# Weighting the experts' rows on their way out and scattering them with adding transfers

## The reference, cut to what matters

```
x   = layernorm(alpha * x + mixer(x))
gp, g  = best of 4 groups (softmax);  e1, e2 = best two of the 4 experts of g, weights ep
combine[token, expert] = gp * ep          # two non-zero entries per token
h   = silu(x @ w_gate[e]) * (x @ w_up[e]) * combine[:, e]
y   = sum over e of h @ w_down[e]
x   = layernorm(alpha * x + y)
```

## Time and profile before

| | |
|---|---|
| median of three executions | 2062.17 us |
| the profiled execution, and its span | 2069.1 us, 2067.4 us |
| PE, VectorE, ACT, POOL busy | 84%, 55%, 43%, 32% |
| read from and written to DRAM | 226.01 MB, 23.23 MB |
| experts, layer 1 and layer 2 | 423.3 to 616.3 us, 1064 to 1258 us |
| second norm, layer 1 and layer 2 | 616.3 to 652 us, 1258.8 to 1296 us |

### The profile page before, as it was taken

The page is one execution under the profiler, slowest core; times in us unless marked ns, Lnnn a source line. Parts: engine busy times, 40 slices in busy tenths (PEclk is TensorE's granted clock), DMA queues, the critical chain, the costliest instruction groups (busy, mean ns, idle before and its releaser), DMA issues. The chain is left out here.

```text
span 2067.4 us, 22445 instructions
## 1 busy us (share of the span) xinstructions
PE 1734.3 (84%) x7990; PEld 1332.7 (64%) x7990; DVE 1138.7 (55%) x1697; ACT 890.2 (43%) x1326; POOL 652.5 (32%) x346
## 2 busy tenths in 40 slices
PE   6999896859971999987859991899697689999997
PEld 4876533748851876732747871788277478888885
DVE  4926565459956745654458985580555424233242
ACT  3246565238853245654327872323635331111111
POOL 2336522112210434632201210343532024444441
PEclk9999997969985999997879996899689899999998
DMA  5201111079944311020147972320000222222211
GB/s 187 74 33 42 42 41 60 15 279 350 372 186 172 108 40 43 1 82 0 62 199 302 376 294 110 144 102 3 20 1 1 82 87 105 94 102 101 93 69 51
DMA packets 40476, 233.84 MB, mean 113 GB/s; under 512 B 9316, under 2 KB 9700, under 8 KB 20660
## 3 DMA queue, kind: packets, MB, share of 16 engines
q1 hardware_dynamic: 31012, 215.44, 27.6%
q0 software_dynamic: 9216, 16.80, 2.2%
q10 hardware_dynamic: 144, 0.26, 0.1%
HBM read 226.01 MB, written 23.23 MB: 121 GB/s over the span
## 5 line engine op out<-in xcount | busy, mean ns | idle before, releaser
L258 PE MATMUL bank<-XS,WS 128*128 128x512 f32 x864 | 200.7, 395 | 11.6 <-DVE WS L383 10.0
L2336 POOL TENSOR_TENSOR WS<-ring,WS 128x2048 fp32r<-128x2048 f32 x31 | 149.6, 4825 | 188.3 <-ACT WS L2324 188.3
L258 PEld LDWEIGHTS bank<-XS,WS 128*128 128x128 f32 x864 | 164.6, 191 | 47.3 <-DVE WS L383 10.5
L1342 PE MATMUL bank<-WS,XS 128*128 128x512 f32 x768 | 188.9, 403 | 1.1 <-DVE XS L1462 1.1
L2357 PE MATMUL bank<-XS,WS 128*128 128x512 f32 x768 | 174.9, 389 | 3.0 <-DVEq L2386 3.0
L2324 ACT CAST WS<-ring 128x2048 fp32r<-128x2048 f32 x31 | 59.3, 1913 | 271.7 <-PE bank L2357 144.0
L2375 PE MATMUL bank<-WS,US 128*128 128x512 f32 x768 | 174.7, 389 | 0.0
L1342 PEld LDWEIGHTS bank<-WS,XS 128*128 128x128 f32 x768 | 146.0, 194 | 32.2 <-DVE XS L1462 1.9
L2357 PEld LDWEIGHTS bank<-XS,WS 128*128 128x128 f32 x768 | 144.1, 188 | 33.1 <-DVEq L2386 3.2
L2375 PEld LDWEIGHTS bank<-WS,US 128*128 128x128 f32 x768 | 144.1, 188 | 29.9
L1687 PE MATMUL bank<-XS,WS 128*128 128x512 f32 (+1 forms) x600 | 139.1, 395 | 3.1 <-POOLq L1738 3.1
(11 more groups left out here) (506 smaller groups left out, 3488.3 us busy)
## 6 DMA issues: line engine op xcount, KB each, us to landing
raw<-in_w_exp SPq DMA_DIRECT2D x16, 2048.0 KB, 13.8
DN<-in_w_exp SPq DMA_DIRECT2D x32, 1024.0 KB
ring<-in_w_ff SPq DMA_DIRECT2D x32, 1024.0 KB, 4.8
raw<-in_w_in SPq DMA_DIRECT2D x20, 1024.0 KB, 4.8
GU<-in_w_exp SPq DMA_DIRECT2D x8, 2048.0 KB, 16.1
XT<-in_w_exp SPq DMA_DIRECT2D x8, 2048.0 KB, 16.4
ring<-in_w_in SPq DMA_DIRECT2D x12, 1024.0 KB, 4.8
raw<-in_w_out SPq DMA_DIRECT2D x8, 1024.0 KB, 5.0
```

What stands on the lines that cost most here:

```text
L258: last = pe.matmul(m.ps[g % 8][:, :], WS[:, i % 2, hw, at:at + P], XS[:, hx, k, :], start=(step == 0), stop=(step == 3 * KD - 1))
L1342: last = pe.matmul(m.ps[2 + e % 2][:, :], r.XS[:, e % 2, hx, 4 * half + k, :], r.WS[:, half, hw, k * S:(k + 1) * S], start=(half == 0 and ...
L2336: pool.tensor_tensor(f.WS[:, q % 2, 1, :], f.ring[:, q % 4, :], f.WS[:, q % 2, 0, :].bitcast(F32), ALU.subtract).then_inc(w_low, 1)
```

## The change

The router computes for each token and expert the weight (0 where the expert is not used) and stores it in VAL as a rounded part and a remainder; VAL grows from two to four numbers, and the target row of the scatter is now the token itself. `index` yields one integer column and, in a second VectorE instruction, the weight WT of each gathered row. ACT brings the down product home multiplied by WT. The scatter adds into `mixed_dram`, which is now 512 rows and starts as a copy of X; since two experts may touch one row, each scatter waits until the one before has landed. The copies of X (`x_rows` as before, and `mixed_dram`) are issued by SP in `norm_stage` as the tiles are finished, all four tiles to `x_rows` first, and POOL waits for all eight before its first gather. The second norm loads 512 KB per tile straight into X and has no additions.

```diff
 norm_stage, SP:
+            for dram in (m.rows_dram, m.mixed_dram):
+                for t in range(NT):
+                    sp.wait_ge(finished, t + 1)
+                    sp.dma_start(dram[t * P:(t + 1) * P, :], m.X[:, t, :]).then_inc(m.rows_out, 16)
 norm_stage, VectorE, finish(t):
-                link(dve.tensor_tensor(m.X[:, t, :], m.X[:, t, :], ln.GB[:, D:2 * D], ALU.add))
+                dve.tensor_tensor(m.X[:, t, :], m.X[:, t, :], ln.GB[:, D:2 * D], ALU.add).then_inc(finished, 1)
 router:
-        @block.sync
-        def _(sp):
-            for t in range(NT):
-                sp.dma_start(m.rows_dram[t * P:(t + 1) * P, :], m.X[:, t, :]).then_inc(copied, 16)
-            sp.wait_ge(copied, 16 * NT)
...
-            link(dve.tensor_tensor(by_group(r.SEC[:, :, :]), every_group(r.h2[:, :, :]), hot_group, ALU.mult))
-            link(dve.tensor_tensor(r.VAL[:, :, :, 1], m.TOK[:, 1, :]..., r.SEC[:, :, :], ALU.add))
...
+            link(dve.tensor_tensor(r.h1[:, :, :], r.h1[:, :, :], wide(r.gm[:, :]), ALU.mult))
+            link(dve.tensor_tensor(r.h2[:, :, :], r.h2[:, :, :], wide(r.m2[:, :]), ALU.mult))
+            link(dve.tensor_tensor(r.h1[:, :, :], r.h1[:, :, :], r.h2[:, :, :], ALU.add))
+            link(dve.tensor_tensor(by_group(r.WV[:, :, :]), every_group(r.h1[:, :, :]), hot_group, ALU.mult))
+            link(dve.tensor_copy(r.VAL[:, :, :, 1], r.WV[:, :, :]))
+            link(dve.tensor_tensor(r.VAL[:, :, :, 2], r.WV[:, :, :], r.VAL[:, :, :, 1].bitcast(F32), ALU.subtract))
+            link(dve.tensor_copy(r.VAL[:, :, :, 3], r.VAL[:, :, :, 0].bitcast(F32)))
 experts, POOL:
             def scatter(e):
                 pool.wait_ge(ye_low, e + 1)
                 pool.wait_ge(ye_up, e + 1)
-                pool.indirect_dma_start(out=m.mixed_dram, out_offset=...(ap=r.TB[:, e, 1:2], axis=0),
-                                        in_=r.YE[:, e % 2, :], in_offset=None, bounds_check=2 * S - 1, oob_is_err=False)...
+                if e:
+                    pool.wait_ge(ye_out[(e - 1) % 2], 16 * ((e - 1) // 2 + 1))
+                pool.indirect_dma_start(out=m.mixed_dram, out_offset=...(ap=r.TB[:, e, 0:1], axis=0),
+                                        in_=r.YE[:, e % 2, :], in_offset=None, bounds_check=S - 1, oob_is_err=False,
+                                        compute_op=ALU.add)...
+            pool.wait_ge(m.rows_out, 16 * 2 * NT)
             gather(0)
 experts, PE:
-                    pe.wait_ge(indexed, e)
+                    pe.wait_ge(weighed, e)
...
-                    last = pe.matmul(m.ps[7][:, 2 * e:2 * e + 2], r.HOT[:, e % 2, t, :], r.VAL[:, t, e, :], ...)
+                    last = pe.matmul(m.ps[7][:, 4 * e:4 * e + 4], r.HOT[:, e % 2, t, :], r.VAL[:, t, e, :], ...)
 experts, ACT:
             def out_home(e):
+                act.wait_ge(weighed, e + 1)
...
-                    act.copy(r.YE[:, e % 2, half * S:(half + 1) * S], m.ps[5 + half][:, :])...
+                    act.mul(r.YE[:, e % 2, half * S:(half + 1) * S], m.ps[5 + half][:, :], r.WT[:, e:e + 1])...
 experts, VectorE:
-                dve.tensor_scalar(r.TB[:, e, :], m.ps[7][:, 2 * e:2 * e + 2], float(NOWHERE), None, ALU.add).then_inc(indexed, 1)
+                dve.tensor_scalar(r.TB[:, e, :], m.ps[7][:, 4 * e:4 * e + 1], float(NOWHERE), None, ALU.add).then_inc(indexed, 1)
+                dve.reduce_sum(r.WT[:, e:e + 1], m.ps[7][:, 4 * e + 1:4 * e + 3], AX.X).then_inc(weighed, 1)
 combine_norm:
-                sp.dma_start(r.MIX[:, t, :], m.mixed_dram.rearrange("(s c) d -> s (c d)", c=2)[t * P:(t + 1) * P, :])...
+                sp.dma_start(m.X[:, t, :], m.mixed_dram[t * P:(t + 1) * P, :])...
...
-                for c, weight in enumerate((r.gm, r.m2)):
-                    link(dve.scalar_tensor_tensor(out=m.X[:, t, :], in0=r.MIX[:, t, c * D:(c + 1) * D], scalar=weight[:, t:t + 1], in1=m.X[:, t, :], ...))
```

More of the change, by code:

```diff
@@ L1151, in router @@
 def router(nc, m, r):
-    names = ("dve_step", "hot_ready", "rank_done", "total_done", "exp_in", "exp_done", "copied")
-    with stage(nc, "router", *names) as (block, (dve_step, hot_ready, rank_done, total_done, exp_in, exp_done, copied)):
-        @block.sync
-        def _(sp):
-            for t in range(NT):
-                sp.dma_start(m.rows_dram[t * P:(t + 1) * P, :], m.X[:, t, :]).then_inc(copied, 16)
-            sp.wait_ge(copied, 16 * NT)
+    names = ("dve_step", "hot_ready", "rank_done", "total_done", "exp_in", "exp_done")
+    with stage(nc, "router", *names) as (block, (dve_step, hot_ready, rank_done, total_done, exp_in, exp_done)):
         @block.gpsimd
@@ L1304, in scatter @@
                 pool.wait_ge(ye_up, e + 1)
-                pool.indirect_dma_start(out=m.mixed_dram, out_offset=bass.IndirectOffsetOnAxis(ap=r.TB[:, e, 1:2], axis=0),
-                                        in_=r.YE[:, e % 2, :], in_offset=None, bounds_check=2 * S - 1, oob_is_err=False).then_inc(ye_out[e % 2], 16)
+                if e:
+                    pool.wait_ge(ye_out[(e - 1) % 2], 16 * ((e - 1) // 2 + 1))
+                pool.indirect_dma_start(out=m.mixed_dram, out_offset=bass.IndirectOffsetOnAxis(ap=r.TB[:, e, 0:1], axis=0),
+                                        in_=r.YE[:, e % 2, :], in_offset=None, bounds_check=S - 1, oob_is_err=False,
+                                        compute_op=ALU.add).then_inc(ye_out[e % 2], 16)
+            pool.wait_ge(m.rows_out, 16 * 2 * NT)
             gather(0)
@@ L1371, in table_of @@
                 if e:
-                    pe.wait_ge(indexed, e)
+                    pe.wait_ge(weighed, e)
                 for t in range(NT):
                     pe.wait_ge(hot_row, e * NT + t + 1)
-                    last = pe.matmul(m.ps[7][:, 2 * e:2 * e + 2], r.HOT[:, e % 2, t, :], r.VAL[:, t, e, :], start=(t == 0), stop=(t == NT - 1))
+                    last = pe.matmul(m.ps[7][:, 4 * e:4 * e + 4], r.HOT[:, e % 2, t, :], r.VAL[:, t, e, :], start=(t == 0), stop=(t == NT - 1))
                 last.then_inc(table_done, 1)
@@ L1416, in out_home @@
                         act.wait_ge(ye_out[e % 2], 16 * (e // 2))
-                    act.copy(r.YE[:, e % 2, half * S:(half + 1) * S], m.ps[5 + half][:, :]).then_inc((ye_low, ye_up)[half], 1)
+                    act.mul(r.YE[:, e % 2, half * S:(half + 1) * S], m.ps[5 + half][:, :], r.WT[:, e:e + 1]).then_inc((ye_low, ye_up)[half], 1)
             def part_high(e):
@@ L1535, in _ @@
             for t in range(NT):
-                sp.dma_start(r.MIX[:, t, :], m.mixed_dram.rearrange("(s c) d -> s (c d)", c=2)[t * P:(t + 1) * P, :]).then_inc(mix_in[t], 16)
+                sp.dma_start(m.X[:, t, :], m.mixed_dram[t * P:(t + 1) * P, :]).then_inc(mix_in[t], 16)
                 if t == 0:
@@ L1555, in _ @@
                 dve.wait_ge(mix_in[t], 16)
-                for c, weight in enumerate((r.gm, r.m2)):
-                    link(dve.scalar_tensor_tensor(out=m.X[:, t, :], in0=r.MIX[:, t, c * D:(c + 1) * D], scalar=weight[:, t:t + 1], in1=m.X[:, t, :], op0=ALU.mult, op1=ALU.add))
                 for half in range(2):
@@ L1573, in square @@
                 act.wait_ge(finished, t + 1)
-                act.activation(r.MIX[:, t, 0:D], m.X[:, t, :], ACT.Square, accum_out=m.SS[:, t:t + 1]).then_inc(squared, 1)
+                act.activation(r.MIX[:, t, :], m.X[:, t, :], ACT.Square, accum_out=m.SS[:, t:t + 1]).then_inc(squared, 1)
             for t in range(NT):
@@ L2583, in build @@
                         r.SEC = sb(nc, c3, "SEC", P, NT, NE)
-                        r.VAL = sbr(nc, c3, "VAL", P, NT, NE, 2)
+                        r.VAL = sbr(nc, c3, "VAL", P, NT, NE, 4)
+                        r.WV = sb(nc, c3, "WV", P, NT, NE)
+                        r.WT = sb(nc, c3, "WT", P, NE)
                         r.HOT = sbr(nc, c3, "HOT", P, 2, NT, P)
@@ L2587, in build @@
                         r.NPI = c3.enter_context(nc.sbuf_tensor("passes", [P, 1], I32))
-                        r.TB = c3.enter_context(nc.sbuf_tensor("table", [P, NE, 2], I32))
+                        r.TB = c3.enter_context(nc.sbuf_tensor("table", [P, NE, 1], I32))
                         with ExitStack() as c4:
@@ L2605, in build @@
                         with ExitStack() as c4:
-                            r.MIX = sb(nc, c4, "MIX", P, NT, 2 * D)
+                            r.MIX = sb(nc, c4, "MIX", P, NT, D)
                             combine_norm(nc, m, ln, r, layer)
-                nums = [s.num for s in (*m.raw_in, m.mla_in, m.out_in)]
+                nums = [s.num for s in (*m.raw_in, m.mla_in, m.out_in, m.rows_out)]
                 nc.all_engine_barrier(sems_to_clear=range(min(nums), max(nums) + 1))
```

12 lines of the change are left out of this document (6 added, 6 removed).

## The result

| | before | after |
|---|---|---|
| median, executions | 2064.02 us, 4 | 2108.6 us, 4 (2100.51 to 2113.55) |
| the profiled execution, its span | 2069.1, 2067.4 us | 2107.12, 2105.3 us |
| experts' stage, layers 1 and 2 | 192.8, 194.3 us | 214.1, 218.8 us |
| second norm, layers 1 and 2 | 37.9, 37.5 us | 27.6, 27.9 us |

Ratio 1.0201, 95% interval 1.0178 to 1.0224: slower by 2.0%, about 41.5 us, where 0.76% (15.6 us) was forecast. The median lies 0.6 us above the end of the range. A stage's length runs from SP's first load of it to SP's first load of the next. By stages of the profiled executions, a layer changes so: from the end of the first norm to the router's first instruction +4.05, router +1.2, experts +21.3 and +24.5, second norm -10.3 and -9.6; in sum +16.2 and +20.1, which makes up the difference of the spans, 37.9, within 1.6 us.

What follows compares the result with a forecast made beforehand. PE set the experts' period of 9.76 us, with the DMA engines' reserve nearly used up. Terms summed to +7.8 us per layer, +15.6 for two: 2084.7 us like the profiled execution, 2078 for a median, range 2050 to 2108; chance 0.38.

Steps and rivals of the forecast that it cites:

- the adding read: Experts' stage: adding costs 0.177 us more per row, 1.04 us per expert on the slowest DMA engine, +12.2 us per layer.
- The new wait: Experts' stage: each scatter waits for the one before, the next gather behind it; put at nothing beyond the DMA term.
- POOL's chain becomes the bound: Rival, experts' stage: adding scatters land in 15.7 us, some 6 us more per expert, about 2173 us; chance 0.12.
- the reserve: Experts' stage: DMA slack before the last weights are used, 0.3 us, taken off the 12.5 of twelve scatters.
- the two small terms: Experts' stage, per layer: PE's waits for the first tables +0.2 us, the last expert's two products with scale +0.2.
- The last scatter: End of the experts' stage: the uncovered last scatter lands 1.1 us later per layer (0.7 to 1.4).
- the rival of the free read: Rival, adding scatters: engines add as fast as they copy, terms 12.2 and 1.1 go, -5.5 per layer, 2051 us; chance 0.27.
- SP's issues: Norm stage: five of SP's eight copy issues come after the last tile and delay the router, +3.1 us per layer.
- The router: Router's chain: two instructions removed, three on 16 elements and four on 64 added, net +1.1 us per layer.
- the second norm: Second norm: two passes per tile go and tile 1's load comes earlier, -10.1 us per layer (-8.8 to -11.8).
- The clock: Rival: the granted clock falls after time without matmuls, making matmuls slower; no total given; chance 0.10.
- The signs named ahead: Expected: software queue's share up by about half, weights' landings past 17 us, experts' stage 13 us longer, second norm 10 shorter.

Runs made afterwards that it cites:

- e3: The kernel after with plain scatters to rows of their own and no wait for the scatter before, part of the sums left out: 2059.24 us, ratio 0.9978 to before.
- e2: The kernel after with adding scatters to a row of its own for each choice and no wait for the scatter before: 2090.04 us, ratio 1.0126 to before.
- e1: The kernel after with plain scatters in place of adding ones, every wait kept: 2069.51 us, ratio 1.0021 to before.
- e5: The kernel after with the gather issued before the scatter that waits: 2100.03 us, ratio 1.0173 to before.
- e10: The kernel after with the gather issued before the scatter and a third buffer for the weighted rows: 2118.93 us, ratio 1.0268 to before.

## Why the prediction was wrong

Direction right, size wrong: 41.5 us instead of 15.6. By the ratios the 26 us missing split into 15.5 for the wait, 4 for the adding read and 6.5 for the rest of the change.

**The step that failed** is "*The new wait*": "A scatter has a full period to land. Before, a gather queued behind its scatter lands 15.7 us after issue at worst, so the scatter alone, first in the ring, needs about half. I put the wait at nothing beyond the DMA term". It costs 15.5 us, 7.8 a layer. The halving had no row under it. In e3 a plain scatter lands after 10.2 us at the median and 13.0 at worst, and after shows 10.8 us at the median for an adding one, against a period of 9.76. The rival "POOL's chain becomes the bound" had the mechanism and the right threshold, "a landing over some 10 us", but priced it at 15.7 + 1 us, over 16 per expert, for 2173. (16.7 less 9.76 is 6.9 us per expert, which its sum rounded down to 6.) Measured are 11.4 to 14.2 us between scatters. The reason that I gave against it works in fact: where POOL is late, the weights' queue gets room (those issued at 588.9 land after 13.0 us, e2's of 588.7 after 20.2), and what the scatters wait for gets shorter (13.3 us for the scatter of 505.60, 10.5 to 11.2 from 545.84 to 592.83). That the wait costs more on top of the addition (15.5 us) than without it (9 us) is not clear of the noise. The rhythms would give it: with the wait a plain chain runs at 10.9 us and an adding one at 12.3, without it e3 runs at 9.74 and e2 at 9.75 and then 11.5.

**The adding read.** 0.22 us a row instead of 0.177. With 0.22 the prediction's own formula gives 64 x 0.22 / 16 x 1.46 = 1.28 per expert, 15.1 for twelve less the reserve; with a tail of 1.4, 16.5. e3 to e2 measured 15.3, forecast were 13.3. Right in mechanism, 4 us too small over two layers. Of the two small terms, the first one shows as PE waiting 5.8 us in three waits for the rows' weights WT, where before it waited 5.0 us for the first table; the scale product can't be told apart in these runs.

**The last scatter** was put at 1.1. Before, the last rows lie ready at 610.52, the scatter is issued at 611.35 and the next stage's load at 616.29. After, they lie ready at 632.52 (631.83 + 0.69), the issue comes at 634.91 since the scatter before is still under way, and the load at 643.11. That is 1.6 more before the issue and 3.3 more from the issue to the load, 4.8 in all. It is part of the two prices above.

**What would have remained without addition and wait** was put at -5.5 a layer (the rival of the free read, -11 us). e3 is that kernel but for one small router instruction: 0.9978, -4.5 us. 1.9 us of this gap are SP's issues, 4.05 a layer instead of 3.1: four stores take 3.73 here, 0.93 each, where I used 0.72 from the router's four and 0.55 from the second norm. The router, 1.2 forecast 1.1, and the second norm, -10.3 and -9.6 forecast -10.1, hold. The other 4 or 5 us lie outside the stages that I followed or within e3's interval.

**The clock.** The mean granted clock in the experts' stages, a mix of its two levels, goes from 0.91 to 0.88, and the busy time of PE in them rises from 166.9 and 166.0 us to 171.5 and 173.2. In e2 it is 0.90, and 168.5 and 169.0; in e1 and e3, whose stages are nearly as short as before, 0.91. So it falls where PE stalls more, and up to 4.5 and 7.1 us of the 21.3 and 24.5 show as slower matmuls. I had this as a rival of its own; it is a part of both prices, and no run takes it away alone.

**The signs named ahead.** Seen: the software queue's share up by half (3.5%), PE waiting on the DMA for rows, second norm 10 us shorter, router late behind SP. Seen only in part: landings past 17 us, which the kernel after reaches once, in layer 1 (17.4 us) and e2 from 511 us on. Not seen: an experts' stage 13 us longer (it is 21 and 24.5) and POOL's waits still ending on ACT alone. The sign against, a scatter waiting on the scatter before it, was the largest wait of the profile.

## What to carry to other kernels

In this kernel an indirect transfer that adds costs over twice the engine time of one that writes (0.40 us a row instead of 0.177), and order among such transfers costs a landing per transfer (10.8 us under load): before making transfers wait for each other, compare the landing under load, not the idle one and not a guess, with the period of the loop. When such a wait appears, another buffer or another order of issues may only move it, as in e5 and e10; shorten the landing. When an indirect transfer uses only the first partitions of its tile, try dealing the filled slots over both halves: it gained 24 us and 6 us in the two kernels here.

## What was not expected of the hardware

- An adding row of 4 KB costs 0.22 us of engine time on top of a plain 0.177, so 0.40: more than a full row's time for the read and the sum.
- Some 64 filled slots of 128, dealt to both halves of the partitions instead of the first, take 24 us off a program of 2108 us without a byte less.
- Adding scatters with hardly any other traffic still need 7.0 us from issue to the next one's issue, 5.4 of it waiting for the landing after the 1.54 us of POOL's instruction. They land after 6.1 to 6.5 us, plain ones in e3 after 3.2 or 3.3. From the last scatter to the next stage's first load it is 8.2 us adding and 4.9 plain.
- A plain scatter that lands after 3.3 us alone lands after 9.1 to 13.0 us beside the loads of the weights (e3).
